# A two-layer encoder trunk on one core: the second mixer's projections, chunk sums and head norms put in another order

## Chip, cores, metric

One Trainium2 chip, one of its cores. The time is the device time of one execution in microseconds (us); lower is better. TensorE is PE in the profile (its weight loads are PEld), VectorE is DVE, ScalarE is ACT, GpSimd is POOL, and SyncE (SP) issues most of the DMAs. Each engine runs its own queue in order; semaphores order the engines among themselves.

## What is computed

x is 512 tokens by 1024 features, f32. Two layers, each a mixer and then a retrieval of single-neuron experts (called peer), with a norm before each. The change lies in the second layer's mixer (gated linear attention, 4 heads) and at its two borders:

```
h = rmsnorm(x)                                    # 512 x 1024
q, k, v, g, z = split(h @ w_in)                   # 512, 512, 1024, 1024, 16 columns
log_a = log_sigmoid(z @ w_gate2 + b_gate2) / 16   # 512 x 512
cum = cumsum of log_a inside each chunk of 64 tokens
k = k * exp(cum[last] - cum)
for chunk c in 0..7, for head:                    # a scan
    state = state * exp(cum[last]) + k_c.T @ v_c  # 128 x 256
    o_c = q_c @ state
o = o * rsqrt(mean(o*o)) * gain * silu(g)         # the norm is per token and head
x = x + o @ w_out
```

## The kernel before, in words

Tokens are four tiles of 128 (`tt`); features are eight blocks of 128 (`kd`). `xnT` holds the normed input turned, features on partitions. PE makes it with eight transposes a tile (`turned(k, tt)`, line 1227), ACT takes half of them out of PSUM (`norm_low`, L499) and DVE the other half (`norm_high`, L774). Before that ACT squares and roots a tile (L492, L494) and DVE scales it (`norm_tile`, L766, L768).

The projections are cut into weight blocks of 1024 x 512 (2 MB), loaded by SP in turns into two slots: `block_load(b)` waits until PE has done the last unit on block b-2 (`used_at`) and then issues one DMA (L370). Block 7 is z, block 8 q, 9 k, 10 and 11 v, 12 and 13 g, 14 and 15 the output projection. A unit is one 128 x 512 result, eight f32 matmuls summed in one of the PSUM banks 0 and 1 in turn: `by_columns` (L1252) gives a result with features on partitions (q, z), `by_tokens` (L1261) one with tokens on partitions (k, v, g; 20 units). ACT takes each out (`unit_out`, L516). PE may start unit j when unit j-2 is out.

At the end of layer 0's peer, `last_group` (L1589) does the last expert products for three token tiles, 24 matmuls each. After each it drains and signals, and DVE adds the products to x (L1182). The transposes of tile 0 for mixer 1 stand after the second tile's products, those of tiles 1 to 3 after the third's.

Mixer 1 then runs on PE: z (eight matmuls that give 16 columns), four matmuls with `w_gate2` (L1432, 17 rows: 16 and the bias), q of four heads, cumulative sums (L1440, L1444), then the 20 units of k, v and g. Only then come the chunk sums: 16 pairs of matmuls over 64 rows (L1461, chunk by chunk, the two heads of a pair one after the other on the same half of the rows), each pair waiting for the scan on DVE (L927, L930, two pairs back), into PSUM banks 2 and 3. Then the readout per token tile (L1472, 64 columns each, the two chunks of a tile in turn), squares on ACT (L636), gating on DVE (L937), one root over all tiles (L639), one reciprocal (L939), 16 scalings (L944), 32 transposes feature block by feature block (L1481), eight evacuations on DVE (L948), and the output projection (L1281, 16 matmuls a token tile) with its adds to x (L798).

`project_out` begins by waiting for both of its blocks, and then runs tile by tile:

```
for dh in range(2):
    arrived(b0 + dh)
```

PE may start half-tile j of it when DVE has added half-tile j-2 (`o_free`). Mixer 0 uses the same function; it transposes its heads 2 and 3 after the first token tile (`other_heads`, L1362), and ACT alone takes those out (L599).

Of the kernel before, what the change touches and what calls it, by code (L numbers as in the profile page):

```python
# [11 lines left out]
ALU = mybir.AluOpType  # L12
# [19 lines left out]
RANK = 16  # L32
TAU = 16.0
PH = 8
# [52 lines left out]
def build(nc, x_d, cols_d, const_d, hot_d, relb_d, wmix_d, wz_d, wg2_d, wq_d, u_d, ur0_d, ur1_d, v0_d, v1_d,  # L87
# [7 lines left out]
    with ExitStack() as ctx:  # L95
# [242 lines left out]
        ends = [4, 8, 12, 16, U0, None, None] + [U0 + n for n in (1, 9, 18, 22, 26, 30, 34)]  # L338
# [4 lines left out]
        def turn_bank(k, tt):  # L343
            if k == 2:
                return 2 * tt
            return 4 + 2 * (tt % 2) if k % 2 else 2 + 2 * (tt % 3)


        @block.sync
        def _(sp):  # L350
# [89 lines left out]
            sp.dma_start(g_w2[0:RANK + 1], wg2_d).then_inc(wg2_in, 16)  # L440
# [13 lines left out]
        def _(pool):  # L454
# [15 lines left out]
            pool.memset(g_z[0:RANK + 1], 1.0).then_inc(pool_prep, 1)  # L470
# [5 lines left out]
        def _(act):  # L476
# [125 lines left out]
            def mixer1():  # L602
                norm(2)
                unit_out(g_z[0:RANK], rows=RANK)
# [11 lines left out]
                for h in range(HEADS):  # L616
# [22 lines left out]
                act.activation(hstd[:], hss[:], ACT.Sqrt, bias=epsc[:], scale=1.0 / DVG).then_inc(hstd_ready, 1)  # L639
# [112 lines left out]
        def _(dve):  # L752
# [161 lines left out]
            def mixer1():  # L914
# [6 lines left out]
                for c in range(NCH):  # L921
                    for h in range(HEADS):
                        n = c * 2 + h // 2
                        dve.wait_ge(kv_done, n + 1)
                        kv = ps[:, 2 + n % 2, (h % 2) * DVG:(h % 2 + 1) * DVG]
                        if c == 0:
                            dve.tensor_copy(g_st[:, c, h], kv).then_inc(st_ready, 1)  # L927
                        else:
                            dve.wait_ge(st_ready, HEADS * (c - 1) + h + 1)
                            dve.scalar_tensor_tensor(g_st[:, c, h], g_st[:, c - 1, h], dcy[:, h, c:c + 1], kv,  # L930
                                                     ALU.mult, ALU.add).then_inc(st_ready, 1)
                for tt in range(TT):
                    dve.wait_ge(go_ss, HEADS * (tt + 1))
                    dve.wait_ge(p_free, U0 + 1 + TT + HEADS + TT + 1 + TT + 2 * TT + 2 * TT)
# [3 lines left out]
                dve.wait_ge(hstd_ready, 3)  # L938
                dve.reciprocal(hrstd[:], hstd[:])  # L939
                dve.drain()  # L940
                for tt in range(TT):
# [20 lines left out]
            def peer(L):  # L962
# [215 lines left out]
                dve.drain().then_inc(x_new, 1)  # L1178
                for tt in range(GT, TT):
# [4 lines left out]
                    closing(L, tt - 1)  # L1184
                closing(L, TT - 1)

            def closing(L, tt):
                if L == 0:
                    norm_tile(2, tt)
                    if tt:  # L1190
                        norm_high(2, tt - 1)
                    if tt == TT - 1:
                        norm_high(2, tt)
                else:
# [508 lines left out]
```

## Time and profile before

| | |
|---|---|
| time, median of 3 runs | 2930.11 us (2928.78 to 2932.38) |
| the profiled execution's own time | 2929.93 us |
| its span, first to last instruction | 2927.8 us |
| PE busy | 2866.0 us (98%) |
| DVE, ACT, POOL busy | 2317.5, 1011.5, 735.9 us |
| mean granted PE clock | 0.993 |
| mixer 1, from z's first matmul to the first of the output projection | 1448.2 to 1678.5 us |

The span lies 2.1 us under the execution's time, and that execution 0.18 us under the median. PE's f32 matmuls show as two instructions each, so a unit of eight has 16.

### The profile page before, as it was taken

To read this page: it belongs to the slowest core of one execution; us is meant where nothing else is said; L and a number is where in the kernel's file an instruction comes from. 1 tells how busy PE (TensorE), PEld (TensorE's weight loads), DVE (VectorE), ACT (ScalarE), POOL (GpSimd) and SP (SyncE) were. 2 spreads that over 40 slices of the span, in tenths; PEclk is the share of its full clock that TensorE was granted. 3 is DMA by queue.
4 is the path that set the end of the run, shared out by engine and by line. 5 is a ranking of instruction groups with operands and counts; after the bars stand their busy time and mean duration, and the time that the engine had idled before them with its cause. 6 is when DMAs were issued, how large, how long until landed. Compare 5 with 4: busy or idle time off the path is not lost.

```text
span 2927.8 us, 39870 instructions
## 1 busy us (share of the span) xinstructions
PE 2866.0 (98%) x14684; PEld 1535.1 (52%) x14684; DVE 2317.5 (79%) x4245; ACT 1011.5 (35%) x1336; POOL 735.9 (25%) x518
## 2 busy tenths in 40 slices
PE   8999999989999999999999899999989999999998
PEld 4456555546666444444444455555556664444443
DVE  6854899998888899999300338999988888999995
ACT  2163232325554333333311123232345543333333
POOL 0000232320113455443000001333301124544540
PEclk9999999999999999999999999999999999999999
DMA  4213677867998999999211126677769989999993
GB/s 153 86 46 138 236 279 264 295 236 258 312 312 310 392 400 398 395 397 369 79 58 58 74 94 231 247 295 267 267 244 309 312 293 394 398 396 393 396 398 114
DMA packets 210410, 775.26 MB, mean 265 GB/s; under 512 B 15445, under 2 KB 97497, under 8 KB 190218
## 3 DMA queue, kind: packets, MB, share of 16 engines
q1 hardware_dynamic: 45698, 416.58, 37.2%
q0 software_dynamic: 73728, 268.47, 25.0%
q10 hardware_dynamic: 90888, 89.14, 8.7%
q8 instruction: 36, 0.59, 0.1%
q14 instruction: 60, 0.49, 0.0%
HBM read 681.59 MB, written 92.54 MB: 264 GB/s over the span
## 4 chain that ended last, share of the span: by engine, by line
PE 69%; DVE 20%; issue 3%; DVEq 2%; ACT 2%; PEld 1%; DMA 1%; PEldq 0%; ACTq 0%; SPq 0%
PE ps L1589 30%; PE ps L1516 6%; PE ps L1517 6%; PE ps L1518 6%; PE ps L1252 5%; DVE arena L987 5%; PE ps L1261 5%; DVE arena L960 4%; PE ps L1281 4%; PE ps L1490 2%; PE ps L1569 2%; PE ps L1568 2%; PEld ps L1589 1%; DVE arena L1071 1%; DVE arena L1075 1%
## 5 line engine op out<-in xcount | busy, mean ns | idle before, releaser
L1589 PE MATMUL ps<-arena 128*128 128x512 bf16 x4608 | 995.6, 379 | 2.7 <-ACT arena L649 2.4
L464 POOL DMA_INDIRECT arena<-in_ur,arena x256 | 336.8, 1316 | 1638.0 <-DVE arena L987 936.6
L1589 PEld LDWEIGHTS ps<-arena 128*128 128x128 bf16 x4608 | 450.5, 98 | 547.3 <-ACT arena L649 3.4
L960 DVE TENSOR_TENSOR arena<-arena 128x1024 bf16<-128x1024 f32 x512 | 612.3, 1220 | 117.7 <-ACT arena L649 108.0
L1516 PE MATMUL ps<-xnh,arena 128*128 128x384 bf16 x2048 | 668.5, 326 | 2.6 <-issue 2.6
L1517 PE MATMUL ps<-xnl,arena 128*128 128x384 bf16 x2048 | 668.6, 326 | 0.0
L1518 PE MATMUL ps<-xnh,arena 128*128 128x384 bf16 x2048 | 668.4, 326 | 0.0
L649 ACT ACTIVATE arena<-arena 128x1024 bf16<-128x1024 f32 x512 | 525.1, 1048 | 177.1 <-PE ps L1589 115.6
L464 POOL DMA_INDIRECT arena<-in_v,arena x256 | 398.2, 1556 | 405.4 <-DVE x_res L996 342.7
L996 DVE SCALAR_TENSOR_TENSOR x_res<-arena,x_res 128x1024 f32<-128x1024 f32 x256 | 328.5, 1283 | 21.1 <-issue 0.9
L987 DVE CUSTOM_DVE_ANT_0 arena<-arena 128x1024 f32<-128x1024 f32 x256 | 305.6, 1218 | 25.2 <-DMA arena<-in_ur,arena 24.5
L675 ACT ACTIVATE arena<-ps 128x384 f32<-128x384 f32 x256 | 125.7, 491 | 530.2 <-PE ps L1518 529.9
L1518 PEld LDWEIGHTS ps<-xnh,arena 128*128 128x128 bf16 x2048 | 200.5, 98 | 133.2 <-issue 1.0
L1516 PEld LDWEIGHTS ps<-xnh,arena 128*128 128x128 bf16 x2048 | 200.4, 98 | 131.5 <-issue 8.0
L711 ACT ACTIVATE arena<-arena 128x1536 bf16<-128x1536 f32 x64 | 94.9, 1483 | 503.0 <-DVEq L1134 503.0
L1517 PEld LDWEIGHTS ps<-xnl,arena 128*128 128x128 bf16 x2048 | 200.5, 98 | 129.3 <-issue 5.3
L1490 PE MATMUL ps<-xnT,arena 128*128 128x512 f32 (+1 forms) x576 | 222.8, 545 | 0.0
L1490 PEld LDWEIGHTS ps<-xnT,arena 128*128 128x128 f32 x576 | 108.9, 190 | 105.4 <-issue 101.4
L1252 PE MATMUL ps<-xnT,arena 128*128 128x512 f32 (+1 forms) x336 | 148.2, 603 | 3.4 <-issue 1.9
L1261 PE MATMUL ps<-arena,xnT 128*128 128x512 f32 x320 | 139.3, 598 | 0.0
L1138 DVE TENSOR_TENSOR arena<-arena 128x1536 bf16<-128x1536 f32 x64 | 112.5, 1758 | 21.9 <-ACT arena L711 21.9
L516 ACT ACTIVATE arena<-ps 128x512 f32<-128x512 f32 (+1 forms) x49 | 29.1, 597 | 265.2 <-PE ps L1252 129.0
(189 smaller groups left out, 2309.8 us busy)
## 6 DMA issues: line engine op xcount, KB each, us to landing
arena<-in_v SPq DMA_DIRECT2D x64, 2048.0 KB, 10.3
arena<-in_u SPq DMA_DIRECT2D x62, 2048.0 KB, 10.2
h_scratch<-arena ACTq DMA_DIRECT2D x60, 768.0 KB
arena<-h_scratch SPq DMA_DIRECT2D x60, 768.0 KB, 8.6
arena<-gate_scratch SPq DMA_DIRECT2D x64, 640.0 KB, 6.9
arena<-in_wmix SPq DMA_DIRECT2D x15, 2048.0 KB, 7.7
gate_scratch<-xnT ACTq DMA_DIRECT2D x10, 2048.0 KB
gate_scratch<-arena ACTq DMA_DIRECT2D x10, 2048.0 KB
```

What stands on the lines that cost most here:

```text
L464: pool.indirect_dma_start(ring[n % NBUF], None, ur_d[L] if g < P else vr_d[L], at).then_inc(gat_in[n % NBUF], 16)
L649: act.activation(hi[:, s], raw[s // TPG][:, s % TPG], ACT.Copy).then_inc(hi_ready, 1)
L960: dve.tensor_tensor(lo[:, s], raw[s // TPG][:, s % TPG], hi[:, s], ALU.subtract).then_inc(lo_ready, 1)
L987: dve.tensor_tensor_reduce(row, row, xg, 1.0, 0.0, ALU.mult, ALU.add, hg[:, g:g + 1]).then_inc(gat_free, 1)
L996: dve.scalar_tensor_tensor(x[:, 0], row, cf[:, g:g + 1], x[:, 0], ALU.mult, ALU.add).then_inc(gat_free, 1)
L1252: last = pe.matmul(bank[0:cols_of], wblk[b % 2][:, kd, at], xnT[:, kd], start=kd == 0, stop=kd == KD - 1)
L1261: last = pe.matmul(bank, xnT[:, kd, at], wblk[b % 2][:, kd], start=kd == 0, stop=kd == KD - 1)
L1490: last = pe.matmul(ps[:, 2 + s, at], wq[:, kd, s * P:(s + 1) * P], xnT[:, kd, at], start=kd == 0, stop=kd == KD - 1)
L1516: pe.matmul(ps[:, j % 2, 0:TD], uh, xnh[:, kd], start=kd == 0, stop=False)
L1517: pe.matmul(ps[:, j % 2, 0:TD], uh, xnl[:, kd], start=False, stop=False)
L1518: last = pe.matmul(ps[:, j % 2, 0:TD], ul, xnh[:, kd], start=False, stop=kd == KD - 1)
L1589: last = pe.matmul(ps[:, 2 + 2 * tt + dh], c, v[:, TPG * s + q, dh * 512:(dh + 1) * 512], start=False, stop=stop and c is cl)
```

## The change

The diff does five things. (1) End of layer 0's peer: tile 0's transposes move into the first tile's products, tile 1's and tile 2's stand after the second's and third's products, tile 3's moves into the mixer; DVE scales tile 0 before its first add, and takes `norm_high` ahead of the next tile's scaling. (2) Mixer 1 starts with q of heads 0 and 1 in two token halves, tile 3's transposes between them; then z, as four column groups of 32 that each sum two of the eight feature blocks; ACT copies all 128 partitions and adds 1 on partition 16, and `w_gate2` is laid four times over 128 rows (256 KB). Heads 2 and 3 of q follow. (3) The chunk sums become eight visits of four matmuls, the two chunks of a token tile in turn on the two row halves, heads 0 and 1 among the units of block 11+1 (`b + 3`), heads 2 and 3 among those of `b + 4`; the readouts stand among those of `b + 4` and `b + 5`. (4) Squares, gating, roots (two, for two tiles each) and scalings go tile by tile, and ACT's go between the g units. (5) The heads are transposed token tile by token tile, 0 and 1 before the output projection, 2 and 3 after its first token tile; DVE and ACT take out one half each. The constants `wz` and `wg2` are laid out to match.

```diff
-        ends = [4, 8, 12, 16, U0, None, None] + [U0 + n for n in (1, 9, 18, 22, 26, 30, 34)]
+        ends = [4, 8, 12, 16, U0, None, None] + [U0 + n for n in (3, 9, 18, 22, 26, 30, 34)]
...
+        def turn_heads(tt):
+            return 6 if tt == TT - 1 else 2
...
-                    sp.dma_start(wblk[b % 2][:, :, 0:RANK], wz_d).then_inc(w_in[b % 2], 16)
+                    sp.dma_start(wblk[b % 2][:, :, 0:ZR], wz_d).then_inc(w_in[b % 2], 16)
...
-            sp.dma_start(g_w2[0:RANK + 1], wg2_d).then_inc(wg2_in, 16)
+            sp.dma_start(g_w2, wg2_d).then_inc(wg2_in, 16)
...
-            pool.memset(g_z[0:RANK + 1], 1.0).then_inc(pool_prep, 1)
+            pool.memset(g_z, 0.0).then_inc(pool_prep, 1)
...
-                unit_out(g_z[0:RANK], rows=RANK)
+                for h in range(2):
+                    unit_out(g_qT[:, h], scale=float(P) ** -0.5)
+                j = unit[0]
+                unit[0] += 1
+                act.wait_ge(p_done, j + 1)
+                act.wait_ge(pool_prep, 2)
+                act.activation(g_z, ps[:, j % 2], ACT.Identity, bias=ident[:, RANK:RANK + 1]).then_inc(p_free, 1)
...
-                for h in range(HEADS):
+                for h in range(2, HEADS):
                     unit_out(g_qT[:, h], scale=float(P) ** -0.5)
...
-                for b in range(2):
-                    for tt in range(TT):
-                        unit_out(g_g[:, tt, b * 512:(b + 1) * 512], ACT.Silu)
-                for tt in range(TT):
+
+                def squares(tt):
...
-                act.activation(hstd[:], hss[:], ACT.Sqrt, bias=epsc[:], scale=1.0 / DVG).then_inc(hstd_ready, 1)
...
+                def heads_root(pair):
...
+                    act.activation(hstd[:, at], hss[:, at], ACT.Sqrt, bias=epsc[:], scale=1.0 / DVG).then_inc(hstd_ready, 1)
...
+                def heads_out(tt):
+                    act.wait_ge(tr_done, TT + tt + 1)
+                    src = ps[:, turn_heads(tt) + 1].rearrange("p (a b t) -> p a b t", a=2, b=2)
+                    dst = g_oT[:, KD // 2:KD, tt * P:(tt + 1) * P].rearrange("p (a b) t -> p a b t", b=2)
+                    for b in range(2):
+                        last = act.activation(dst[:, :, b], src[:, :, b], ACT.Copy, scale=cols[:, C_GLAG + b:C_GLAG + b + 1])
+                    last.then_inc(tr_free, 1)
+
+                for n in range(2 * TT):
+                    b, tt = n // TT, n % TT
+                    unit_out(g_g[:, tt, b * 512:(b + 1) * 512], ACT.Silu)
+                    if n == 1:
+                        squares(0)
+                    if n == 2:
+                        squares(1)
+                    if n == 5:
+                        heads_root(0)
+                        squares(2)
+                    if n == 6:
+                        squares(3)
+                        heads_out(0)
+                heads_root(1)
+                for tt in range(1, TT):
+                    heads_out(tt)
...
-                for c in range(NCH):
-                    for h in range(HEADS):
-                        n = c * 2 + h // 2
-                        dve.wait_ge(kv_done, n + 1)
-                        kv = ps[:, 2 + n % 2, (h % 2) * DVG:(h % 2 + 1) * DVG]
-                        if c == 0:
-                            dve.tensor_copy(g_st[:, c, h], kv).then_inc(st_ready, 1)
-                        else:
-                            dve.wait_ge(st_ready, HEADS * (c - 1) + h + 1)
-                            dve.scalar_tensor_tensor(g_st[:, c, h], g_st[:, c - 1, h], dcy[:, h, c:c + 1], kv,
-                                                     ALU.mult, ALU.add).then_inc(st_ready, 1)
-                for tt in range(TT):
+                def states(n):
+                    hp, i = n // TT, n % TT
+                    dve.wait_ge(kv_done, n + 1)
...
+                                                         ALU.mult, ALU.add).then_inc(st_ready, 1)
+
+                def gated_heads(tt):
...
-                    dve.wait_ge(p_free, U0 + 1 + TT + HEADS + TT + 1 + TT + 2 * TT + 2 * TT)
...
-                for tt in range(TT):
+
+                def scale_heads(tt):
+                    if tt % 2 == 0:
+                        at = slice(HEADS * tt, HEADS * (tt + 2))
+                        dve.wait_ge(hstd_ready, 3 + tt // 2)
+                        dve.reciprocal(hrstd[:, at], hstd[:, at])
+                    dve.drain()
                     for h in range(HEADS):
                         g = g_g[:, tt, h * DVG:(h + 1) * DVG]
                         dve.tensor_scalar(g, g, hrstd[:, tt * HEADS + h:tt * HEADS + h + 1], None,
                                           ALU.mult).then_inc(heads_ready, 1)
-                for kd in range(KD):
-                    dve.wait_ge(tr_done, HEADS + kd + 1)
-                    dve.tensor_scalar(g_oT[:, kd], ps[:, 2 + kd % 2], cols[:, C_GLAG + kd % 2:C_GLAG + kd % 2 + 1], None,
-                                      ALU.mult).then_inc(tr_free, 1)
+
+                def heads_out(tt):
+                    dve.wait_ge(tr_done, TT + tt + 1)
+                    src = ps[:, turn_heads(tt)].rearrange("p (a b t) -> p a b t", a=2, b=2)
+                    dst = g_oT[:, 0:KD // 2, tt * P:(tt + 1) * P].rearrange("p (a b) t -> p a b t", b=2)
+                    for b in range(2):
+                        last = dve.tensor_scalar(dst[:, :, b], src[:, :, b], cols[:, C_GLAG + b:C_GLAG + b + 1], None, ALU.mult)
+                    last.then_inc(tr_free, 1)
+
+                for n in range(2 * TT):
+                    states(n)
+                gated_heads(0)
+                gated_heads(1)
+                scale_heads(0)
+                scale_heads(1)
+                gated_heads(2)
+                heads_out(0)
+                gated_heads(3)
+                scale_heads(2)
+                scale_heads(3)
+                for tt in range(1, TT):
+                    heads_out(tt)
                 project_out(1)
...
+                if L == 0:
+                    norm_tile(2, 0)
                 for tt in range(GT, TT):
                     dve.wait_ge(out_done, DT * L + tt)
                     xp = x[:, tt].rearrange("p (a b) -> p a b", a=2)
                     dve.tensor_tensor(xp, xp, ps[:, 2 * tt:2 * tt + 2], ALU.add).then_inc(x_new, 1)
                     dve.drain()
-                    closing(L, tt - 1)
-                closing(L, TT - 1)
-
-            def closing(L, tt):
+                    if L == 0:
+                        norm_high(2, tt - 1)
+                        norm_tile(2, tt)
+                    else:
+                        closing(tt - 1)
...
+                    norm_high(2, TT - 1)
...
-                                pe.wait_ge(tr_free, HEADS + KD * m)
+                                pe.wait_ge(tr_free, HEADS + 2 * TT * m)
...
-                    if tt == 0 and between:
+                    if tt == 0:
                         between()
...
-                b = Z_BLOCK
-                pe.wait_ge(pool_prep, 2)
-                by_columns(b, 0, RANK)
+                b = Z_BLOCK + 1
+
+                def q_half(bank, h, at):
+                    for kd in range(KD):
+                        last = pe.matmul(bank[:, at], wblk[b % 2][:, kd, h * P:(h + 1) * P], xnT[:, kd, at],
+                                         start=kd == 0, stop=kd == KD - 1)
+                    return last
+
+                halves = slice(0, T // 2), slice(T // 2, T)
+                pe.wait_ge(xt_low, TT * 2 + 2)
+                pe.wait_ge(xt_high, TT * 2 + 2)
+                arrived(b)
+                q_banks = unit_bank(), unit_bank()
+                q_half(q_banks[0], 0, halves[0])
+                turned(2, TT - 1)
+                q_half(q_banks[1], 1, halves[0])
+                all_turned(2)
+                for h in range(2):
+                    q_half(q_banks[h], h, halves[1]).then_inc(p_done, 1)
+
+                arrived(Z_BLOCK)
+                bank = unit_bank()
+                for kd in range(KD):
+                    at = slice(kd % 4 * ZR, (kd % 4 + 1) * ZR)
+                    last = pe.matmul(bank[at], wblk[Z_BLOCK % 2][:, kd, 0:ZR], xnT[:, kd], start=kd < 4, stop=kd >= 4)
+                last.then_inc(p_done, 1)
                 pe.wait_ge(p_free, unit[0])
                 pe.wait_ge(wg2_in, 16)
                 for tt in range(TT):
                     bank = unit_bank()
-                    pe.matmul(bank, g_z[0:RANK + 1, tt * P:(tt + 1) * P], g_w2[0:RANK + 1], start=True, stop=True).then_inc(p_done, 1)
-                b += 1
-                for h in range(HEADS):
+                    pe.matmul(bank, g_z[:, tt * P:(tt + 1) * P], g_w2, start=True, stop=True).then_inc(p_done, 1)
+                for h in range(2, HEADS):
                     by_columns(b, h)
 
                 pe.wait_ge(nla_ready, 1)
@@ -1445,25 +1530,22 @@
                                          const[:, K_IND:K_IND + 2], start=True, stop=True)
                 last.then_inc(p_done, 1)
...
-                for _ in range(5):
-                    b += 1
-                    for tt in range(TT):
...
+                def chunk_sums(n):
+                    hp, i = n // TT, n % TT
+                    if n:
+                        pe.wait_ge(st_ready, 4 * n)
+                    else:
+                        pe.wait_ge(kdec_ready, TT)
+                    for h in (2 * hp, 2 * hp + 1):
+                        for c in (2 * i, 2 * i + 1):
+                            at = slice(c % 2 * CHUNK, (c % 2 + 1) * CHUNK)
+                            last = pe.matmul(ps[:, 2 + c % 2, (h % 2) * DVG:(h % 2 + 1) * DVG],
+                                             g_k[at, i, h * P:(h + 1) * P], g_v[at, i, h * DVG:(h + 1) * DVG],
                                              start=True, stop=True)
-                        last.then_inc(kv_done, 1)
-                for tt in range(TT):
-                    pe.wait_ge(st_ready, HEADS * 2 * (tt + 1))
+                    last.then_inc(kv_done, 1)
+
+                def readout(tt):
+                    pe.wait_ge(st_ready, 4 * (TT + tt + 1))
                     if tt >= 2:
                         pe.wait_ge(go_out, 2 * (tt - 1))
...
+                def heads(tt):
+                    pe.wait_ge(heads_ready, 16 + HEADS * (tt + 1))
+                    if tt == 1 or tt == 2:
+                        pe.wait_ge(tr_free, HEADS + 2 * tt)
+                    for kd in range(KD):
+                        at = kd % (KD // 2) * P
+                        last = pe.transpose(ps[:, turn_heads(tt) + kd // (KD // 2), at:at + P], g_g[:, tt, kd * P:(kd + 1) * P], ident)
                     last.then_inc(tr_done, 1)
-                project_out(1, b + 1, g_oT, [(kd, tr_free, (HEADS + kd + 1, 0, 0, 0)) for kd in range(KD)])
+
+                for tt in range(TT):
+                    by_tokens(b + 1, tt)
+                for tt in range(TT):
+                    by_tokens(b + 2, tt)
+                for tt in range(TT):
+                    by_tokens(b + 3, tt)
+                    if tt == 0:
+                        pe.wait_ge(p_free, U0 + 14 + TT + TT)
+                    chunk_sums(tt)
+                for tt in range(TT):
+                    by_tokens(b + 4, tt)
+                    if tt == 0:
+                        pe.wait_ge(p_free, U0 + 14 + TT + 2 * TT)
+                    chunk_sums(TT + tt)
+                    if 1 <= tt < 3:
+                        readout(tt - 1)
+                for tt in range(TT):
+                    by_tokens(b + 5, tt)
+                    if 1 <= tt < 3:
+                        readout(tt + 1)
+                    if tt == 2:
+                        heads(0)
+                heads(1)
+                pe.wait_ge(p_free, unit[0])
+
+                def other_heads():
+                    heads(2)
+                    heads(3)
+
+                project_out(1, b + 6, g_oT, [(kd, tr_free, (6, 8, 12, 12) if kd == 0 else (0, 0, 0, 0)) for kd in range(KD)],
+                            other_heads)
 
...
-                        if tt < DT - 1:
-                            pe.drain().then_inc(out_done, 1)
-                        if tt == 1 and L == 0:
-                            turned(2, 0)
-                    pe.drain().then_inc(out_done, 1)
-                    if L == 0:
-                        for tt in range(GT, TT):
+                            if L == 0 and tt == 0 and q == 1:
+                                turned(2, 0)
+                        pe.drain().then_inc(out_done, 1)
+                        if L == 0 and tt:
                             turned(2, tt)
-                        all_turned(2)
```

## Rows read from the trace of the kernel before

**Rows 1.** The page: the chain that ended last, by engine.

```profile
PE 69%; DVE 20%; issue 3%; DVEq 2%; ACT 2%; PEld 1%; DMA 1%; PEldq 0%; ACTq 0%; SPq 0%
```

**Rows 2.** Mixer 1 in stretches: length, PE, PEld, DVE, ACT, POOL busy; clock; DMA share, GB/s.

```profile
1498.00:1637.90 139.90, 139.21 (x322) 61.23 (x321) 2.77 (x4) 13.42 (x22) 0.00 (x0) 0.99 0.16 60
1654.40:1668.70 14.30, 7.51 (x65) 4.68 (x64) 6.69 (x14) 9.19 (x34) 0.00 (x0) 1.00 0.00 1
```

**Rows 3.** The chain of work, 1400 to 1700 us: start, us, what.

```profile
1441.50 1.22 DVE x_res L1182
...
1443.05 0.75 DVE arena L768
...
1445.83 0.67 PE ps L1227 x4
...
1448.19 7.04 PE ps L1252 x16
1455.25 0.60 ACT arena L516
...
1460.57 29.36 PE ps L1252 x64
...
1637.24 0.61 ACT arena L516
...
1678.49 20.60 PE ps L1281 x48
```

**Rows 4.** The chain, first 320 us: query halves, and one tile's transposes.

```profile
257.50 3.45 PE ps L1490 x16
260.99 1.06 PE ps L1227 x8
262.05 10.36 PE ps L1490 x48
```

**Rows 5.** Timeline around the chunk sums, the readouts and the heads.

```profile
1637.89 16.52 PE L1461 MATMUL ps<-arena 64*128 64x256 f32 x64 [0.69 <-ACT arena L516]
1659.94 1.95 PE L1472 MATMUL ps<-arena 128*64 128x256 f32 x16 [1.93 <-DVE arena L937]
1659.91 1.52 PEld L1472 LDWEIGHTS ps<-arena 128*64 128x64 f32 x16 [2.35 <-issue]
1666.36 1.28 ACT L639 ACT_TABLE_LOAD   x1
```

**Rows 6.** Timeline of PE in mixer 0, matmuls on alternate row halves.

```profile
186.52 1.13 PE L1317 MATMUL ps<-arena 64*128 64x512 f32 x4
187.58 1.98 PE L1357 MATMUL ps<-arena 128*128 128x512 f32 x4
```

**Rows 7.** The load of block 15 by itself, L370: issues, and time to landing.

```profile
L370 SPq DMA_DIRECT2D arena<-in_wmix x1: 328/328/328, 1637.2 to 1637.2; - x1
...
DMA to landing us min/median/max: 7.7/7.7/7.7
```

**Rows 8.** The granted clock in short stretches, columns as in rows 2.

```profile
1460.00:1462.00 2.00, 1.71 (x3) 0.84 (x3) 0.00 (x0) 1.94 (x4) 0.00 (x0) 0.62 0.96 410
1462.00:1464.00 2.00, 2.00 (x3) 0.67 (x2) 0.00 (x0) 1.99 (x2) 0.00 (x0) 0.53 0.03 8
178.00:186.00 8.00, 8.00 (x37) 4.24 (x37) 5.14 (x16) 3.35 (x11) 0.00 (x0) 1.00 0.00 0
```

**Rows 9.** Groups of instructions on ACT and DVE, 1400 to 1720 us.

```profile
L492 ACT ACTIVATE arena<-x_res 128x1024 f32<-128x1024 f32 x6 | 6.4, 1063 | 45.5 <-DVEq L801 32.0 <-DVE x_res L1182 11.7 <-DVEq L1178 1.9
...
L944 DVE TENSOR_SCALAR arena<-arena,hrstd 128x256 f32<-128x256 f32 x16 | 4.3, 348 | 0.1
...
L927 DVE COPY arena<-ps 128x256 f32<-128x256 f32 x4 | 1.5, 420 | 110.5 <-PE ps L1461 110.4
```

**Rows 10.** Timeline in mixer 0's output projection, first to second token tile.

```profile
212.63 1.04 PE L1362 MATMUL ps<-const,arena 128*128 128x128 f32 x8
213.51 7.03 PE L1281 MATMUL ps<-arena 128*128 128x512 f32 x16
```

More of the change, by code:

```diff
@@ L32 @@
 RANK = 16
+ZR = 32
 TAU = 16.0
+GLA_KEYS = 512
 PH = 8
@@ L937, in mixer1 @@
                         dve.tensor_tensor(g, g, ps[:, 4 + 2 * (tt % 2) + b], ALU.mult).then_inc(go_out, 1)
-                dve.wait_ge(hstd_ready, 3)
-                dve.reciprocal(hrstd[:], hstd[:])
-                dve.drain()
-                for tt in range(TT):
+                def scale_heads(tt):
[4 more added lines that the diff above has]
+                    dve.drain()
                     for h in range(HEADS):
@@ L1262, in by_tokens, with project_out @@
                 last.then_inc(p_done, 1)
-            def project_out(m, b0, src, order, begun=0, between=None):
+            def project_out(m, b0, src, order, between, begun=0):
                 for dh in range(2):
@@ L1421, in mixer0 @@
                 project_out(0, 5, m_cat, [(CT + ct, conv_out, (ct + 1, 0, 0, 0)) for ct in range(CT)]
-                            + [(h, tr_free, (1, 2, 4, 4)) for h in range(HEADS)], begun=CT, between=other_heads)
+                            + [(h, tr_free, (1, 2, 4, 4)) for h in range(HEADS)], other_heads, begun=CT)
             def mixer1():
-                b = Z_BLOCK
-                pe.wait_ge(pool_prep, 2)
-                by_columns(b, 0, RANK)
+                b = Z_BLOCK + 1
[21 more added lines that the diff above has]
+                last.then_inc(p_done, 1)
                 pe.wait_ge(p_free, unit[0])
@@ L1475, in mixer1 @@
                     last.then_inc(go_done, 1)
-                for kd in range(KD):
-                    for tt in range(TT):
-                        pe.wait_ge(heads_ready, 16 + HEADS * tt + kd // 2 + 1)
-                        if kd >= 2 and tt == 0:
-                            pe.wait_ge(tr_free, HEADS + kd - 1)
-                        last = pe.transpose(ps[:, 2 + kd % 2, tt * P:(tt + 1) * P], g_g[:, tt, kd * P:(kd + 1) * P], ident)
-                    last.then_inc(tr_done, 1)
-                project_out(1, b + 1, g_oT, [(kd, tr_free, (HEADS + kd + 1, 0, 0, 0)) for kd in range(KD)])
+                def heads(tt):
[5 more added lines that the diff above has]
+                        last = pe.transpose(ps[:, turn_heads(tt) + kd // (KD // 2), at:at + P], g_g[:, tt, kd * P:(kd + 1) * P], ident)
+                    last.then_inc(tr_done, 1)
+                for tt in range(TT):
[9 more added lines that the diff above has]
+                    by_tokens(b + 4, tt)
+                    if tt == 0:
+                        pe.wait_ge(p_free, U0 + 14 + TT + 2 * TT)
[15 more added lines that the diff above has]
+                            other_heads)
             def peer(L):
@@ L1677 @@
                            blocks(w_odd[:, :3072]), blocks(arr("odd_w_out")[0])])
-    wz = w_odd[:, 3072:].reshape(KD, P, RANK).transpose(1, 0, 2)
-    wg2 = np.concatenate([arr("w_gate2")[0], arr("b_gate2")])
+    wz = np.zeros((P, KD, ZR), f32)
+    wz[:, :, 0:RANK] = w_odd[:, 3072:].reshape(KD, P, RANK).transpose(1, 0, 2)
+    wg2 = np.zeros((P, GLA_KEYS), f32)
+    for g in range(P // ZR):
+        wg2[ZR * g:ZR * g + RANK] = arr("w_gate2")[0]
+    wg2[RANK] = arr("b_gate2")[0]
     wq = arr("peer_w_query").reshape(2, KD, P, PH, 2 * P).transpose(0, 3, 2, 1, 4).reshape(2, PH, P, -1)
```

42 lines of the change are left out of this document (18 added, 24 removed).

## The prediction

> **What bounds the kernel now.** I read the page first. PE is busy for 98% of the span (the table above) and holds 69% of the chain that ended last [rows 1], so only PE's own time and its gaps count; the gaps in mixer 1 are too short for the page's slices. Next came the same stretches one by one, and the chain through them. The 20 units of k, v and g take 139.21 us of PE, 6.96 each (6.87 in a steady stretch, by the q heads: see the clock below), while DVE works 2.8 us of 140 and ACT 13.4 [rows 2]: two idle engines under a full one. From 1637.24 to 1678.49 the chain is made of the scan, readouts, squares, root, scalings and transposes, 41.25 us in which none of the big projections runs [rows 3]. PE is busy there only in part (7.5 of 14.3 us in the readout stretch [rows 2]). The third place is the border before: DVE adds the last products at 1441.50, z starts only at 1448.19 and takes 7.04 us, and w_gate2 with its evacuations lasts to 1460.57 [rows 3].
>
> **The border.** Before, z starts 6.69 us after the last add begins [rows 3]. After, three sets of transposes stand before or directly behind the third tile's products: one more than before, 0.9 us (a set holds PE for 1.06 us alone [rows 4], and some 0.87 in a stream), so these products end at 1442.4 and tile 2's transposes at 1443.4. Tiles 0 and 1 are in xnT by then (their DVE and ACT parts run under the products), and the first q half starts at 1443.5, to 1447.0 (3.45 [rows 4]). Meanwhile tile 3 is added from 1442.5 (1.22 [rows 3]), squared (1.06 [rows 9]) and rooted, 1.6 together, and scaled (a reciprocal and 0.75 [rows 3], 1.0): ready at 1446.4, with 0.6 us to spare. Its transposes take 1.06, and the other three halves 10.36 [rows 4]: q of two heads is done at 1458.4. Before, the same two heads would take 13.73 from 1448.19, to 1461.9. The border gives 3.5 us.
>
> **z.** Eight matmuls of 512 columns in 7.04 us now, 0.44 for each of 16 instructions [rows 3]. In four column groups, if four run at once: 1.76, and 0.2 for entering and leaving, 2.0 us. The nearest row is the readout, which alternates two column halves: 16 instructions of 256 columns in 1.95 us, 0.12 each where one after the other would be 0.22 [rows 5]. So halves overlap fully; four groups are not shown, and the bound above is the 7.04 of no overlap. I take 2.0: a gain of 5.1. The weight loads of the readout are busy 1.52 us inside its 1.95 [rows 5], thus beside matmuls of the other half. The Trainium skill ("TensorE: Matmul & The Clock Gate", Part 3, on packing small matmuls) states that weight loads overlap matmuls in flight only where the row group differs. By that rule z's 16 loads, at the 0.10 us of each of the readout's, would come on top, 1.6 us, and the total would be 2912; the trace does not agree for column halves. ACT's copy of z over 128 rows instead of 16 has the same 512 elements a row, w_gate2's matmuls the same columns: both cost nothing new. ACT must first take out q of head 1 (0.6 us), which is over before z ends. The bigger w_gate2 load is issued at 1442, some 18 us before its use. Block 9's load now waits for the later z: issued at 1460.4, landed after 7.7 [rows 7] at 1468, wanted after w_gate2 (5.3), two q heads (13.7) and the cumulative sums (8.1: from the end of the q heads at 1489.9 to 1498), at about 1487. The DVE sum and the decays keep their place behind w_gate2. So at the start of the k units the gain is 8.6 us.
>
> **Chunk sums.** Sixteen pairs, 16.52 us, 2.07 for each four matmuls of 256 columns [rows 5]. In the new order the row halves alternate. The nearest row is mixer 0's four instructions on alternate row halves, 512 columns: 1.06 us until the next work starts [rows 6], where four at 0.43 would need 1.72; two at a time 0.85, and 0.21 more for entering and leaving. A chunk visit has as many columns: 1.06 us, eight 8.5. The bound above is no overlap, 8 x 2.07 = 16.5. The scan of a visit (four operations on DVE near L927's 0.42 [rows 9]) lies under the next unit of 6.87; if that cover were gone it would come back as before. The row's 0.21 is what a visit in the stream costs. The Trainium skill ("TensorEngine Tiling (Array Packing)", Key Properties) says that changing the tiling mode drains TensorE; the row agrees, with 0.21 for a visit, and it speaks against this change, which goes in and out 13 times. Without that drain the sum would be 2.7 us lower.
>
> **Readouts and heads.** Four readouts of 1.95 [rows 5]: 7.8. Their squares (9.19 us of ACT for four tiles and the root [rows 2], so 2.3 a tile at most) stand between g units 6.87 apart; ACT then needs at most 0.6 + 2.3 + 1.1 and two table loads of 1.28 [rows 5], 6.6 us, against 9.9 between units with a readout and a chunk visit. Gating and scaling on DVE hide likewise; heads 0's scalings are ready 3.8 us after the second unit of the last block, its transposes come 8 us after. They cost 0.87.
>
> **A new wait.** `project_out` waits for both its blocks. Block 15's load waits in SP's queue for the last g unit (used_at), at 1637.24, and lands 7.7 us later [rows 7]. Today 41 us of heads hide it. After the change PE has only heads 1's transposes (0.9) left to do, then it stands until 7.8 us after its last g unit, 6.9 idle. All that is queued behind on PE is the whole projection and peer 1. DVE uses the wait: gating of tile 3 (under 1.7: 6.69 us of DVE for four tiles and more [rows 2]), one reciprocal, eight scalings (0.27 each [rows 9]) and half of tile 1's heads are over 6.2 us after the last unit, before the block lands. peer 1's first query weights go behind block 15 in SP's queue, as before.
>
> **Clock.** From 1461 to 1464 the granted clock was 0.62 and 0.53, so PE was partly at 1.2 GHz, after a stretch of short matmuls with waits; the first q head paid 29.36 - 4 x 6.87 = 1.9 us [rows 3, 8]. I let this stay where it is (q's third head) and let the new idle of 6.9 us cost the projection the same: 1.9.
>
> **A new bubble.** After the first token tile PE transposes heads 2 and 3 (2 x 0.87). In mixer 0 the next matmul follows at once, 0.88 us behind the start of the transposes [rows 10], for DVE has nothing but adds in its queue. Now DVE's queue has `heads_out(2)` and `heads_out(3)` ahead of the first add, and the next half tile needs that add. Heads_out is two evacuations of 256 elements a row, near L927's 0.42 [rows 9]. So 0.9 for heads 3 after its transposes, the add 0.69, signals 0.3: a bubble of 1.9 us. Bounds: nothing, and 3.5.
>
> **The sum.** After the last k and v work: 8.5 + 7.8 + 0.9 + 7.8 (wait, heads 1 inside) + 1.9 + 1.7 + 1.9 = 30.5, instead of 41.25: 10.7 gained. With 8.6, 19.3 us. From the profiled execution's 2929.93 that gives 2910.6, call it 2911; the median shown is 0.18 above that execution. Peer 1 begins earlier by as much and is unchanged: its loads start at the projection's end as before.
>
> **Rivals.**
> - *No wait for block 15*, or so little that it hides: minus 6.9 and the 1.9 of clock, 2902. For it speaks only that I may have missed slack; the landing time and the queue are against it. 10%.
> - *Row halves do not overlap* for chunk sums (256 columns, 8 loads a visit): plus 8.1, 2919. Rows 6 are against it. 12%.
> - *Column groups of z do not overlap four deep*: plus 5, 2916. 6%.
> - *The clock falls at visits*: each fall costs 1.9. With half of 12 visits, plus 11: 2922; with all, 2934. Mixer 0's visits every 4 us ran at 1.00 [rows 8], and f32 units stand between. 10%.
> - *Nothing comes of it*: the scan's order still holds PE at every visit, because DVE or ACT is late, and the 41 us stay, stretched out: 2924 to 2931. Against it: DVE and ACT are idle for over nine tenths of the units' time [rows 2]. 4%.
> - *Slower*: PE drops to 1.2 GHz at the first chunk visit and stays there through the 12 units it is mixed with. Each then takes 6.87 more, 82 in all, about 2993. It decides from 3.7 such units on (25 us over my sum). 3%.
> My forecast as it stands has 55%, its own range 2906 to 2916.
>
> **Range and chances.** From the first rival's 2902 less 1 for the bubble's lower bound, to row halves' 2919 with 2 for a further fall of clock: 2901 to 2921, which holds the forecast, the first three rivals and part of the fourth. A measurement here tells about 0.2% (5.9 us) from no change. Faster by more than that, under 2924: 93%; within: 4%; slower: 3%.
>
> **What would show it.** Chunk visits of about 1.06 us and z of 2.0; the first q half started about 1443.5 and the k units 8.6 us earlier; PE idle for about 7 us ahead of the output projection, released by the DMA of in_wmix; a gap near 1.9 us before its second token tile, released by DVE's add. It would be wrong if units of g start late behind ACT, if the visits run at 2 us, or if the clock row shows more than the known falls.

## The result and the profile after

The changed kernel takes 2910.60 us (median of 4 runs, 2910.07 to 2911.53), the kernel before in the same comparison 2929.47 us (4 runs): ratio 0.9934, 95% interval 0.9921 to 0.9947, so 15.5 to 23.1 us faster. The forecast was 2911 in 2901 to 2921.

The chain of work of the changed kernel, 1400 to 1720 us (start, us, what); L1492 is a q half, L1512 z, L1315 q, L1529 the small sums, L1324 a unit, L1542 a chunk visit, L1554 a readout, L1565 the heads' transposes, L1344 the projection:

```profile
1441.00 1.09 PE ps L1290 x8
1442.09 3.46 PE ps L1492 x16
1445.54 0.87 PE ps L1290 x8
1446.41 10.36 PE ps L1492 x48
1456.78 1.90 PE ps L1512 x16
...
1464.13 13.99 PE ps L1315 x32
...
1482.68 4.52 PE ps L1529 x32
1487.21 64.30 PE ps L1324 x144
1551.50 1.06 PE ps L1542 x8
1552.57 7.06 PE ps L1324 x16
...
1592.14 1.06 PE ps L1542 x8
1593.21 1.88 PE ps L1554 x16
1595.09 7.06 PE ps L1324 x16
...
1613.22 13.93 PE ps L1324 x32
1627.15 1.88 PE ps L1554 x16
1629.03 7.06 PE ps L1324 x16
...
1638.99 6.88 PE ps L1324 x16
```

Against [rows 3]: PE goes from tile 2's transposes into the first q half at once, z takes 1.90 us for 7.04, and the k units start at 1487.2 for 1498.07. All eight chunk visits take 1.06 us. The first unit behind each visit takes 7.06 us, one that follows a unit 6.87 (13.93 for two).

The timeline of all engines but the weight loads around the start of the projection:

```profile
1645.70 1.04 PE L1565 MATMUL ps<-const,arena 128*128 128x128 f32 x8
1645.89 0.33 SPq L376 DMA_DIRECT2D arena<-in_wmix  x1
...
1646.60 1.29 DVE L977 TENSOR_TENSOR arena<-arena,ps 128x512 f32<-128x512 f32 x2 [6.69 <-ACT arena L522]
...
1648.42 2.38 DVE L987 TENSOR_SCALAR arena<-arena,hrstd 128x256 f32<-128x256 f32 x8
1650.72 0.87 DVE L995 TENSOR_SCALAR arena<-ps,cols 128x256 f32<-128x256 f32 x2
1654.02 16.52 PE L1344 MATMUL ps<-arena 128*128 128x512 f32 x32 [7.28 <-issue]
1670.37 1.91 PE L1565 MATMUL ps<-const,arena 128*128 128x128 f32 x16
...
1671.44 1.75 DVE L995 TENSOR_SCALAR arena<-ps,cols 128x256 f32<-128x256 f32 x4 [19.86 <-PE ps L1565]
1673.11 1.27 DVE L836 TENSOR_TENSOR x_res<-x_res,ps 128x512 f32<-128x512 f32 x2
1673.85 1.55 PE L1344 MATMUL ps<-arena 128*128 128x512 f32 x3 [1.57 <-DVE x_res L836]
```

and the load issued at 1645.89, by itself:

```profile
DMA to landing us min/median/max: 7.9/7.9/7.9
```

PE ends its last unit, transposes heads 1 and stands 7.28 us. The trace names no releaser ("issue"), but the load of block 15 goes out at 1645.89 and lands 7.9 later, at 1653.8, 0.2 us ahead of the projection, and DVE is done at 1651.6. Later PE waits 1.57 us for DVE's first add, which stands behind four evacuations. The clock (columns as in [rows 2]):

```profile
1483.00:1487.00 4.00, 4.00 (x30) 4.00 (x30) 0.00 (x0) 0.32 (x1) 0.00 (x0) 0.76 0.41 172
1487.00:1489.00 2.00, 2.00 (x4) 0.97 (x5) 0.00 (x0) 0.20 (x1) 0.00 (x0) 0.50 0.00 0
...
1600.00:1646.00 46.00, 46.00 (x161) 21.30 (x160) 10.53 (x25) 12.37 (x35) 0.00 (x0) 1.00 0.12 46
1646.00:1654.00 8.00, 0.74 (x7) 0.51 (x6) 4.56 (x13) 2.81 (x5) 0.00 (x0) 0.68 0.87 335
1654.00:1656.00 2.00, 1.98 (x3) 0.97 (x4) 0.00 (x0) 0.00 (x0) 0.00 (x0) 0.50 0.71 300
```

It stays at 1.00 (2.4 GHz) through the visits and falls to 0.50 (1.2 GHz) in two places: at the small sums, and in the wait for block 15, after which the projection's first token tile takes 16.52 us for 13.73.

### The profile page after: what moved, and what is told of

The parts are those of the page before. It is cut to its first block, busy times and chain, and to the rows that moved or that the text cites. A ratio compares the mean times of both kernels' runs of the same rounds, so it can differ in the third digit from the quotient of the medians.

```text
span 2908.2 us, 39928 instructions
## 1 busy us (share of the span) xinstructions
PE 2851.8 (98%) x14716; PEld 1532.3 (53%) x14716; DVE 2315.6 (80%) x4246; ACT 1017.2 (35%) x1347; POOL 734.6 (25%) x518
## 4 chain that ended last, share of the span: by engine, by line
PE 71%; DVE 20%; DVEq 3%; issue 2%; DMA 2%; ACT 1%; PEld 1%; PEldq 0%; POOL 0%; ACTq 0%
PE ps L1704 32%; PE ps L1631 6%; PE ps L1632 6%; PE ps L1633 6%; DVE arena L1048 5%; PE ps L1324 5%; PE ps L1315 4%; PE ps L1344 4%; DVE arena L1021 4%; PE ps L1605 2%; DMA arena<-in_ur,arena 2%; PE ps L1684 2%; PE ps L1683 1%; DVE arena L1132 1%; DVE arena L1136 1%
## 5 line engine op out<-in xcount | busy, mean ns | idle before, releaser
L1605 PE MATMUL ps<-xnT,arena 128*128 128x512 f32 (+1 forms) x576 | 222.8, 545 | 0.0
L1324 PE MATMUL ps<-arena,xnT 128*128 128x512 f32 x320 | 142.5, 604 | 0.0
L1315 PE MATMUL ps<-xnT,arena 128*128 128x512 f32 x288 | 124.1, 593 | 2.3 <-issue 2.0
L522 ACT ACTIVATE arena<-ps 128x512 f32<-128x512 f32 x48 | 28.5, 596 | 252.1 <-PE ps L1324 127.5
```

The costliest lines, as they stand in the source:

```text
L1315: last = pe.matmul(bank[0:cols_of], wblk[b % 2][:, kd, at], xnT[:, kd], start=kd == 0, stop=kd == KD - 1)
L1324: last = pe.matmul(bank, xnT[:, kd, at], wblk[b % 2][:, kd], start=kd == 0, stop=kd == KD - 1)
L1605: last = pe.matmul(ps[:, 2 + s, at], wq[:, kd, s * P:(s + 1) * P], xnT[:, kd, at], start=kd == 0, stop=kd == KD - 1)
```

## The experiments

Three measures: the median; the ratio to the kernel before, measured on the same chip; and, free of what the start and the end add by chance, the stretch in each profiled execution from the first peer's first query matmul to the second peer's (255.31 to 1717.78 us in the changed kernel). The stretch has chance of its own: in the nine kernels that are alike up to the end of q's heads 0 and 1, the way there from the first query matmul takes 1199.3 to 1201.8 us.

| kernel | median us | ratio, 95% interval | stretch us |
|---|---|---|---|
| before | 2929.47 | | 1478.55 |
| changed | 2910.60 | 0.9934, 0.9921 to 0.9947 | 1462.47 |
| start only | 2920.22 | 0.9965, 0.9953 to 0.9978 | 1470.84 |
| tail only | 2920.50 | 0.9972, 0.9963 to 0.9982 | 1472.81 |
| z plain | 2917.36 | 0.9956, 0.9939 to 0.9972 | 1468.09 |
| whole q | 2915.63 | 0.9952, 0.9936 to 0.9969 | 1466.66 |
| row order of before | 2909.06 | 0.9927, 0.9910 to 0.9943 | 1459.52 |
| drained halves | 2918.88 | 0.9965, 0.9953 to 0.9978 | 1470.48 |
| filled wait | 2909.30 | 0.9928, 0.9911 to 0.9945 | 1460.98 |
| split wait | 2899.48 | 0.9902, 0.9885 to 0.9918 | 1449.09 |
| add first | 2907.68 | 0.9931, 0.9914 to 0.9948 | 1458.32 |
| split wait, add first | 2897.28 | 0.9890, 0.9873 to 0.9906 | 1449.01 |

**The start only**: `mixer1` from the k units on is that of before, on all engines.

> Only the first half of the change: the peer's end, the q halves, z in column groups; from the k units on everything as before (all 20 units, then chunk sums, readouts, heads, projection). Theory: 8.6 us of the gain are here, 2921 us (2919.5 to 2922.5), and the k units start that much earlier. Rival (the units hide it, or the clock's fall comes at another place and takes it back): 2925 or more.

Ratio 0.9965: 6.4 to 13.8 us gained, 10.3 in the middle; by the stretch 7.7. My 8.6 lies between, 2925 does not fit. The k units start at 1487.46, as in the changed kernel.

**The tail only**: z, q and the peer's end as before; the rest as changed.

> Only the second half of the change: the peer's end, z and q as before; chunk sums, readouts, head norms and the projection as changed. Theory (the two halves of the gain add up; the first half alone gave about 9.5 to 10): 7.5 to 9.5 us gained, 2920 to 2922, with 7.1 us idle before the projection. Rival (my sum's 10.7 for this part): 2918.5 to 2919.5. Second rival (the parts overlap, each would give most of the gain alone): 2914 or less.

Ratio 0.9972: 8.2 us gained (5.3 to 10.8); by the stretch 5.7, with 7.02 us idle ahead of the projection, and z itself at the low clock in this execution (8.95 us for 7.03). The two parts give 18.5 together by their ratios, the whole 19.3: they add up. The 10.7 of my sum for this part is at the edge of the interval, and over what the trace shows: from the k units to the second peer 229.6 us for 238.0, so 8.4.

**z plain**, one column group:

```diff
-                    at = slice(kd % 4 * ZR, (kd % 4 + 1) * ZR)
-                    last = pe.matmul(bank[at], ...[:, kd, 0:ZR], xnT[:, kd], start=kd < 4, stop=kd >= 4)
+                    last = pe.matmul(bank[0:ZR], ...[:, kd, 0:ZR], xnT[:, kd], start=kd == 0, stop=kd == KD - 1)
```

> The changed kernel, with z summed in one column group of 32 (eight matmuls into the same partitions, one after the other) and w_gate2's matmuls over 32 rows. Theory: z takes 6.9 to 7.0 us instead of 1.9, plus 5.0, 2915.6; the granted clock may move, plus or minus 1. Rival (block 9 or the decays end later anyway, so z's time is not on the path): plus 0 to 1, 2911.

The timeline of PE:

```profile
1455.96 7.05 PE L1511 MATMUL ps<-xnT,arena 128*32 128x512 f32 x16
...
1468.87 16.60 PE L1315 MATMUL ps<-xnT,arena 128*128 128x512 f32 x32
...
1489.88 3.73 PE L1528 MATMUL ps<-const,arena 128*128 128x2 f32 x32
```

7.05 us instead of 1.90, and 5.6 in the stretch; 6.4 by the ratio. A fall of the clock is back as well: q's heads 2 and 3 take 16.60 us for 13.97, as q paid in the kernel before. The plus or minus 1 that I allowed for the clock came out as 2.6 here, against 1.6 less than in the changed kernel in and behind the small sums (3.73 and nine units of 63.74, for 4.68 and 64.44).

**Whole q**: no halves.

```diff
...
-                q_half(q_banks[0], 0, halves[0])
                 turned(2, TT - 1)
-                q_half(q_banks[1], 1, halves[0])
                 all_turned(2)
                 for h in range(2):
-                    q_half(q_banks[h], h, halves[1]).then_inc(p_done, 1)
+                    by_columns(b, h)
```

> The changed kernel, with tile 3's transposes right after tile 2's and q of heads 0 and 1 over all tokens at once, so that PE waits until all four tiles are in xnT. Theory (the half over tokens 0 to 255 hides the add, root, scaling, transposes and evacuations of tile 3): PE stands some 4 to 5 us (from 1442 to about 1447), plus 3.5 to 5 us, 2915. Rival (the border gained by the DVE order alone and the halves give nothing): plus under 1, 2911.

```profile
1439.91 1.09 PE L1290 MATMUL ps<-const,arena 128*128 128x128 f32 x8
1443.74 1.10 PE L1290 MATMUL ps<-const,arena 128*128 128x128 f32 x8 [2.74 <-DVE arena L806]
1446.10 16.91 PE L1315 MATMUL ps<-xnT,arena 128*128 128x512 f32 x32 [1.27 <-ACT xnT L505]
```

In PE's timeline the waits are back, 2.74 and 1.27 us, and with them a low clock in q (16.91 for 13.97). Ratio plus 0.0018, 5.3 us; the stretch plus 4.2. As expected in size, but made up otherwise. From the first peer's first query to z it is 6.0 us more (1207.4 for 1201.4), 2.9 of it the clock; the small sums and the nine units behind them, at less of the low clock, give 1.7 back. So the halves hide tile 3, some 3 us, and PE stays at 2.4 GHz with them.

**Row order of before** inside a visit:

```diff
-                    for h in (2 * hp, 2 * hp + 1):
-                        for c in (2 * i, 2 * i + 1):
+                    for c in (2 * i, 2 * i + 1):
+                        for h in (2 * hp, 2 * hp + 1):
```

> The changed kernel, with the four matmuls of a chunk visit in the order of before: two heads on one row half, then two on the other. Theory (neighbours on different row halves run at the same time): a visit takes about 1.7 to 2.1 us instead of 1.06, eight visits plus 5 to 8 us, 2916 to 2919. If only the middle pair overlaps, three steps of 0.43 and 0.2: 1.5 us, plus 3.5, 2914. Rival (the gain comes from leaving the wait for the scan alone): 1.06 us still, 2910.6.

This missed. PE's timeline shows a visit as long as before the edit:

```profile
1550.68 1.14 PE L1542 MATMUL ps<-arena 64*128 64x256 f32 x8
1551.75 7.13 PE L1324 MATMUL ps<-arena,xnT 128*128 128x512 f32 x16
```

So the order of neighbours does nothing (the stretch is 3.0 us shorter than the changed kernel's: 1.7 of it the clock behind the small sums, 1.0 in the first peer, so chance of an execution). But that left two readings: the halves never overlap, as the rival has it, or they overlap whenever both stand in one visit.

**Drained halves**: the same order, and PE drained between the halves.

```diff
+                    for c in (2 * i, 2 * i + 1):
+                        if c % 2:
+                            pe.drain()
+                        for h in (2 * hp, 2 * hp + 1):
```

> The changed kernel, chunk visits in the order one row half first, then the other, with a drain of PE between the halves, so that the two can't be in work together. Theory (the halves run at the same time wherever both stand in one visit, whatever their order): a visit takes 1.9 to 2.2 us instead of 1.06, eight visits plus 7 to 9, 2918. Rival (a matmul over 64 rows is short by itself, and the gain was only the wait for the scan): 1.2 to 1.4 us a visit, plus 1 to 3, 2912.

PE's timeline:

```profile
1562.54 2.33 PE L1544 MATMUL ps<-arena 64*128 64x256 f32 x8
1564.80 7.13 PE L1324 MATMUL ps<-arena,xnT 128*128 128x512 f32 x16
```

It is 2.26 us to the next unit, for 1.06; eight times 1.20 is 9.6, the ratio rises by 0.0031 (9.1 us), the stretch by 8.0, less than 9.6 mainly because the projection's first token tile takes 15.36 us here instead of 16.52. What the drain itself costs is in the 1.20. The weight loads of one visit tell the two apart, first drained, then in the changed kernel:

```profile
1553.21 0.73 PEld L1544 LDWEIGHTS ps<-arena 64*128 64x128 f32 x4 [0.76 <-issue]
1554.41 0.73 PEld L1544 LDWEIGHTS ps<-arena 64*128 64x128 f32 x4 [0.48 <-issue]
...
1559.56 0.73 PEld L1542 LDWEIGHTS ps<-arena 64*128 64x128 f32 x8 [0.76 <-issue]
```

One half's four loads take 0.73 us, and both halves' eight take 0.73 us too when nothing stands between them (0.74 in the row order of before). So the halves do run together, and of the 1.20 us 0.73 is the second half's own turn and 0.47 the drain. Before, each pair sat on one half and waited for the scan, so there was nothing to run beside it.

**Filled wait**: work for PE while block 15 loads; its results are read by nobody.

```diff
                 heads(1)
+                pe.wait_ge(go_out, 6)
+                for _ in range(44):
+                    pe.matmul(ps[:, 4, 0:TD], xnh[:, 0, 0:P], xnh[:, 1], start=True, stop=True)
```

> The changed kernel, with 44 bf16 matmuls of 384 columns (7.2 us at full clock) whose results nobody reads, put after heads 1's transposes, so that PE is busy while block 15 loads. Theory (the first token tile is slow because PE had been idle before it and the granted clock had fallen): the first token tile takes 13.8 to 14.2 us instead of 16.5, the granted clock is 1.00 through it, and the whole is 2 to 2.8 us under the changed kernel, 2908. Rival (it is slow for another reason, the load of the block beside it for one): 16.5 us still, and 2910.6 to 2911.5.

```profile
1648.24 1.04 PE L1565 MATMUL ps<-const,arena 128*128 128x128 f32 x8
1649.11 7.31 PE L1593 MATMUL ps<-xnh 128*128 128x384 bf16 x44
1657.25 13.97 PE L1344 MATMUL ps<-arena 128*128 128x512 f32 x32 [0.82 <-issue]
```

The first token tile takes 13.97 us, at a granted clock of 1.00. So the other 2.55 were the clock. From heads 1's transposes to the second peer it is 70.2 us, for 72.1; the load took 8.5 us here, which is why not all of the 2.55 shows. The whole gains 1.3 us at the median, under the 2 to 2.8 expected, and the runs can't tell the two apart.

**Split wait**:

```diff
-                for dh in range(2):
-                    arrived(b0 + dh)
                 for tt in range(TT):
                     for dh in range(2):
                         b = b0 + dh
+                        if tt == 0:
+                            arrived(b)
```

> The changed kernel, but the output projection waits for block 14 ahead of its first half tile and for block 15 ahead of its second, not for both at the start. My theory (the wait for block 15 is on the path): the first half tile (6.87 us) runs inside the 7.9 us that block 15 needs to land; idle before the projection falls from 7.3 us to under 0.3, some 0.9 stays before the second half tile, and the 2.8 us that the first token tile takes over 13.73 goes too. Together 8.5 to 9.5 us under the changed kernel, about 2901.5 us. Rival (the time is given back in the second peer, whose gathers and loads set its pace): under 2 us gained, 2909 to 2911. Second rival (the slow first token tile comes from something else than the idle): about 6.5 us gained, 2904.

```profile
1642.49 1.04 PE L1565 MATMUL ps<-const,arena 128*128 128x128 f32 x8
1643.36 14.18 PE L1344 MATMUL ps<-arena 128*128 128x512 f32 x32
```

In PE's timeline the projection follows the transposes without a gap, and its first tile takes 14.18 us (13.90 later), so that 0.3 is left of the 0.9 us that I expected ahead of its second half. From the transposes to the second peer it is 62.3 us for 72.1, 9.8 gained, and 0.0032 of the ratio is 9.4. That settles what the trace did not name: the wait is block 15's, it is on the path, and it brings the clock's fall with it. Nothing is given back in the second peer: from its first query to the end it takes 1191.0 us here, 1190.4 in the changed kernel.

**Add first**: DVE adds the first half tile ahead of heads 2 and 3.

```diff
-                for tt in range(1, TT):
-                    heads_out(tt)
-                project_out(1)
+                heads_out(1)
+                project_out(1, late_heads)   # heads_out(2), heads_out(3) behind the first add
```

> The changed kernel, with DVE adding the first half tile of the projection before it takes out heads 2 and 3, not after. My theory (PE waits for DVE's add before the second token tile because two evacuations stand ahead of it in DVE's queue): the gap of 1.57 us goes, 2909 us. Rival (the gap moves to the next half tile, which needs the second add, now behind the evacuations): nothing gained, 2910.6.

```profile
1668.07 1.91 PE L1571 MATMUL ps<-const,arena 128*128 128x128 f32 x16
1669.81 7.03 PE L1350 MATMUL ps<-arena 128*128 128x512 f32 x16
```

The gap is gone in PE's timeline and does not come back at the next half tile: 70.0 us from heads 1's transposes to the second peer, 2.0 less. At the median 2.9 less, by the ratio 0.9; the intervals are too wide for it, the trace is not.

**Both**:

> Both edits, the split wait and the add first. Theory: they add up, 10 to 11 us under the changed kernel, about 2900 us. Rival (the queue behind the late block shifts so that DVE's evacuations are the new bound): no better than the split wait alone, 2901.5.

60.5 us from transposes to peer for 72.1: 11.6, close to the two effects' sum (9.8 and 2.0). The stretch hides the second effect, because the way from the first query matmul to z took 1.7 us longer here than in the split wait (1201.2 for 1199.5). 2897.28 us, ratio 0.9890: the best version, 13.3 us under the changed kernel at the median.

**The kernel before, again**:

> The kernel before, a second profiled execution. Theory (of the 19.6 us between the two profiled spans only about 16 lie between the two peers' first query matmuls, 1478.55 us before and 1462.47 after; the rest is chance of one execution, at the start above all, where the clock rose 1.7 us sooner in the one after): that stretch again 1478 to 1479 us, while the second peer to the end takes 1190.5 to 1192. Rival (the change also quickens the second peer by 1.5 us): 1191.9 again for the kernel before, and no other kernel of this one's like under it.

The stretch is 1479.19 us (255.62 to 1734.81), the second peer to the end 1191.4. The stretch repeats within 0.6 us in this pair, though equal parts of other kernels differ by more (1199.3 to 1201.8 above). What differs more is the start: the first query matmul comes at 255.3 to 255.7 in some executions and at 257.2 to 257.5 in others, of either kernel. The rival is not out, however. From its first query to the end the second peer takes 1191.4 to 1192.0 us in the three profiles with the mixer's end as before (this kernel twice, and the start only) and 1190.3 to 1191.1 in the ten with the changed end. About 0.9 us of the gain may lie there; why is open.

## Why the prediction was right

**Border** (3.5 us): right. From the end of the third products to q's end it took 15.9 us, 16.0 by my steps (1442.4 to 1458.4); counted from the first peer's first query, q's end came 3.1 us earlier than my 1461.9 for the kernel before.

**z** (2.0 us, four groups at once): right, 1.90. The weight loads did not come on top: the 16 are 0.11 us each and together are busy for 0.42 us only. By the Trainium skill's rule on them ("TensorE: Matmul & The Clock Gate", Part 3) my estimate would be 3.5 us, and the trace does not bear it out for column groups either.

**Chunk visits** (1.06 us each): right in size, and the overlap that it took for granted is shown by the drained halves and their weight loads. My reading of the 2.07 us before was incomplete: I put it down to neighbours on one half; it was the wait between pairs that kept the halves apart, and the order of neighbours is free.

**Entering and leaving** (0.21 a visit): too low. The visit has it, and the unit behind it pays another 0.19 us (7.06 for 6.87), nine times, 1.7 us that my sum left out. The Trainium skill's rule that a change of the tiling mode drains TensorE ("TensorEngine Tiling (Array Packing)", Key Properties) agrees with both, though no run separates a drain from another cost of the change.

**The new wait** (7.8 us from the last unit): right, 8.1, and shown by the split wait.

**Clock** (1.9 after the wait): mis-sized, 2.8 us. The fall at q, which I had left where it was, is gone (13.99 us for two heads): 1.6 us that I did not count. It comes back with z plain and with whole q. In whole q waits of PE stand ahead of it; in z plain PE was busy until z's end and then waited no longer than in the changed kernel, so idle time alone does not explain it, and the cause is open. The fall at the small sums, which I had overlooked, is there in every kernel: 1.8 us before (139.15 less 20 x 6.87), and 3.4 in the changed kernel's profile (4.52 less 3.56, and 64.30 less 61.83). The one paid for the other here by chance: kernels with the same start paid 1.8 in three profiles (split wait, both, row order of before) and 3.4 in five.

**The bubble** (1.9): right, 1.57, and 0.26 in the half tile behind it.

**The sum**: the stretch gained 16.1 us, not 19.3. Counted from the first peer's first query, the k units start 8.8 us earlier (8.6 by my sum). So the missing 3.4 are in the tail, 7.25 us for 10.7: 1.7 behind the visits, 0.7 and 0.9 of clock (in the first nine units, and after the wait), 0.35 of wait, 0.26 behind the bubble, with small terms of either sign. Where the small sums paid 1.8 only, the tail of otherwise like kernels gained 7.9 to 8.4, so 10.7 was too much without that chance as well; the step that was mis-sized is entering and leaving, 1.7 us, then the clock. Of the 19.6 us between the two profiled spans 2.0 lie ahead of the stretch and 1.5 in the second peer. At the medians the gain is 18.9, with an interval of 15.5 to 23.1 that holds both numbers, so that 2911 met 2910.6 so closely is partly chance.

## What to carry to other kernels

Where serial work of idle engines is put under a busy TensorE, ask which load was hidden by the serial work: here 8.1 us of the hidden 41 came back as a wait for the last weight block, and one wait split per half took it off. Put a transfer's wait at the first instruction that reads it, and an addition that frees a bank ahead of evacuations that nobody waits for yet. Small matmuls on two row halves or four column groups ran together here where they stood in one stretch with no wait between; a pair on one half that waits has nothing to run beside.

## What the runs showed of the hardware

- Four f32 matmuls of 64 rows and 256 columns on two row halves take 1.06 us in either order, 2.26 with a drain between the halves. Their eight weight loads take 0.73 us, as long as the four of one half.
- Eight f32 matmuls of 512 columns in four column groups of 32 take 1.90 us, in one group 7.05.
- A unit behind a row-half or column-half stretch takes 7.06 us, behind a full one 6.87.
- PE was busy all through the small sums (two columns each, 3.56 us at full clock), and still the granted clock fell to 1.2 GHz in them or behind them in every kernel here, at 1.8 us in eight profiles and 3.4 in five. PE had waited 0.78 us for ACT ahead of the last two matmuls before them, so no run shows which of the two it was. The clock did not fall at the visits of 64-row and 64-column matmuls.
- The rise of the clock at the start varies between executions: the first 256 f32 matmul instructions took 110.12 us in nine profiles and 111.72 or 111.81 in four, and the granted clock over the first 60 us was 1.00 or 0.97.
